# Expert loop of a mixture-of-experts layer: the scaling of the gathered rows moves from VectorE to GpSimd, as a multiplication and an addition

## What is computed

```python
h2 = rms(x, p['g_ffn']) * (1 + sc2) + sh2
aff = softmax(h2 @ w_router)
gate, idx = top_k(swapaxes(aff, 1, 2), cap)        # 64 latent rows, 16 context rows
xg = h2[idx]
a  = xg @ w_e1                                     # 2048 -> 1024
g3 = xg @ w_e3
y  = ((silu(a) * g3) @ w_e2) * gate                # 1024 -> 2048
x  = x + gate2 * zeros.at[idx].add(y)
```

## Time and profile before

| | before |
|---|---|
| median of three runs | 3317.91 us |
| the profiled execution | 3315.78 us |
| its span, first to last instruction | 3313.7 us |
| TensorE busy (share of the span) | 3235.8 us (98%) |
| VectorE busy | 2121.0 us (64%) |
| ScalarE busy | 1391.5 us (42%) |
| GpSimd busy | 358.4 us (11%) |
| granted TensorE clock, mean | 0.991 |

### The profile page before, as it was taken

One profiled execution on the slowest core, in us unless ns is written; L12 is line 12 of the kernel. 1 busy time (PEld: TensorE's weight loads), 2 busy tenths in 40 slices (PEclk: granted clock), 3 DMA queues, 4 the chain that ended last, 5 costly groups with the idle time before them and its releaser, 6 DMA issues. The chain is left out here.

```text
span 3313.7 us, 39738 instructions
## 1 busy us (share of the span) xinstructions
PE 3235.8 (98%) x15947; PEld 2506.7 (76%) x15947; DVE 2121.0 (64%) x1875; ACT 1391.5 (42%) x1271; POOL 358.4 (11%) x445
## 2 busy tenths in 40 slices
PE   7999999999999999999999999969999999999997
PEld 4888888888888999998888888746666666666664
DVE  4355565565552777773233243279999999999997
ACT  3221222221212445452121222247777777777775
POOL 0020010020000000001101112100111111111102
PEclk9999999999999999999999999979999999999999
DMA  9575555485553110125353455379999999999999
GB/s 398 215 230 176 202 178 175 159 271 197 186 187 119 38 48 34 40 101 207 133 172 135 151 172 191 127 256 373 388 398 396 388 384 387 396 393 385 389 391 338
DMA packets 143918, 787.25 MB, mean 238 GB/s; under 512 B 19888, under 2 KB 30672, under 8 KB 63936
## 3 DMA queue, kind: packets, MB, share of 16 engines
q1 hardware_dynamic: 101344, 666.40, 52.2%
q0 software_dynamic: 42448, 119.03, 12.1%
HBM read 718.11 MB, written 67.25 MB: 237 GB/s over the span
## 5 line engine op out<-in xcount | busy, mean ns | idle before, releaser
L102 DVE TENSOR_TENSOR w_lo<-w_stage,w_hi 128x2048 fp32r<-128x2048 f32 x379 | 863.5, 2287 | 95.9 <-ACT w_hi L97 94.7
L97 ACT ACTIVATE w_hi<-w_stage 128x2048 fp32r<-128x2048 f32 x379 | 727.4, 1920 | 299.7 <-PE e_ps L109 299.7
L107 PE MATMUL i_ps<-w_hi,hT_hi 128*128 128x512 f32 (+1 forms) x1440 | 563.0, 391 | 0.1
L109 PE MATMUL i_ps<-w_hi,hT_lo 128*128 128x512 f32 (+1 forms) x1440 | 554.7, 385 | 0.0
L108 PE MATMUL i_ps<-w_lo,hT_hi 128*128 128x512 f32 (+1 forms) x1440 | 554.5, 385 | 0.0
L107 PE MATMUL e_ps<-w_hi,xgT_hi 128*80 128x512 f32 x1024 | 404.3, 395 | 0.0
L108 PE MATMUL e_ps<-w_lo,xgT_hi 128*80 128x512 f32 x1024 | 403.2, 394 | 0.0
L109 PE MATMUL e_ps<-w_hi,xgT_lo 128*80 128x512 f32 x1024 | 400.6, 391 | 0.0
L599 DVE TENSOR_TENSOR w_lo<-w_raw,w_hi 128x2048 fp32r<-128x2048 f32 (+1 forms) x72 | 161.7, 2246 | 345.6 <-ACT w_hi L458 345.6
L107 PE MATMUL p_ps<-w_hi,xT_hi 128*128 128x512 f32 x960 | 377.9, 394 | 1.4 <-DVEq L1841 1.4
L109 PE MATMUL p_ps<-w_hi,xT_lo 128*128 128x512 f32 x960 | 374.1, 390 | 0.0
(11 more groups left out here) (365 smaller groups left out, 4490.9 us busy)
## 6 DMA issues: line engine op xcount, KB each, us to landing
w_stage<-in_w_e SPq DMA_DIRECT2D x384, 1024.0 KB, 7.4
w_stage<-in_w_ada SPq DMA_DIRECT2D x96, 1024.0 KB, 7.1
w_raw<-in_w_in SPq DMA_DIRECT2D x64, 1024.0 KB, 5.0
w_stage<-in_w_o_gm SPq DMA_DIRECT2D x16, 1024.0 KB, 7.4
w_stage<-in_w_o_mla SPq DMA_DIRECT2D x16, 1024.0 KB, 5.1
w_stage<-in_w_out SPq DMA_DIRECT2D x16, 1024.0 KB, 5.0
acts<-evacuated POOLq DMA_DIRECT2D x60, 256.0 KB, 4.4
side<-acts POOLq DMA_DIRECT2D x40, 256.0 KB, 5.5
```

Source lines behind the costliest of these rows:

```text
L97: act.activation(dst, src, ACT.Copy).then_inc(st.hi, 1)
L102: dve.tensor_tensor(dst, src, hi.bitcast(F32), ALU.subtract).then_inc(st.split, 1)
L107: pe.matmul(out, x_hi, w_hi, start=first, stop=False)
L109: return pe.matmul(out, x_lo, w_hi, start=False, stop=last)
```

## The change

VectorE's calls of `rows_scaled` in the loop are removed. GpSimd gets a function of the same name that waits for the gather and then, for each of the three groups of columns, multiplies the rows by their factor (`tensor_scalar`), waits for that, and adds the shift (`tensor_tensor`). It runs after `columns_of(i)` and before `gather(i + 3)`, for experts 2 to 15. TensorE's wait on `x_sc` is as it was. The whole diff:

```diff
--- before.py
+++ after.py
@@ -2063,7 +2063,7 @@
             sem(f"e_{n}") for n in ("x_tr", "x_hi", "x_lo", "sil_ok", "hid_ok", "h_tr", "h_hi", "h_lo", "y_ev"))
         inv, ex, ex_inv, aff_ok, aff_tr, backs, picked, picks, pick_tr, pick_ok = (
             sem(f"r_{n}") for n in ("inv_rows", "ex", "ex_inv", "aff_ok", "aff_tr", "backs", "picked", "picks", "pick_tr", "pick_ok"))
-        shift_in, x_sc, inv_out, issued = sem("r_shift_in"), sem("e_x_scaled"), M.pool_sem("r_inv_out"), sem("r_issued")
+        shift_in, x_sc, x_mul, inv_out, issued = sem("r_shift_in"), sem("e_x_scaled"), sem("e_x_times"), M.pool_sem("r_inv_out"), sem("r_issued")
         f_in, f_out, g_in = [M.pool_sem(f"f_in{b}") for b in range(N_F)], [M.pool_sem(f"f_out{b}") for b in range(N_F)], sem("f_g_in")
         f_sq, f_sum, f_var, f_std, f_inv, f_ok, rows_y_ok, last_out = (
             *(sem(f"f_{n}") for n in ("sq", "sum", "var", "std", "inv", "ok", "rows")), M.pool_sem("last_out"))
@@ -2137,6 +2137,16 @@
                 if e == 0:
                     pool.memset(cur_g[:], 0).then_inc(issued, 1)
 
+            def rows_scaled(e):
+
+                pool_wait(pool, gathered, 16 * e + 16, passed)
+                for g in range(3):
+                    a, b = TXG[g]
+                    c = slice(a * P, b * P)
+                    pool.tensor_scalar(xg[:, c], xg[:, c], xg[:, D:D + 1], None, ALU.mult).then_inc(x_mul, 1)
+                    pool_wait(pool, x_mul, 3 * e + g - 5, passed)
+                    pool.tensor_tensor(xg[:, c], xg[:, c], shift[:, c], ALU.add).then_inc(x_sc, 1)
+
             def columns_of(e):
 
                 pool.tensor_copy(cur_gate[:], gates[:, bass.ds(e, 1)]).then_inc(idx_s, 1)
@@ -2158,10 +2168,13 @@
                 gather_first(e)
             with pool.Fori(0, EXPERTS - 3) as i:
                 columns_of(i)
+                rows_scaled(i + 2)
                 gather(i + 3)
                 scatter(i)
             for e in range(LAST - 2, LAST):
                 columns_of(e)
+                if e + 2 < EXPERTS:
+                    rows_scaled(e + 2)
                 scatter(e)
 
             def load_x(t):
@@ -2368,8 +2381,6 @@
                     lo(n0 + j + LEAD, j + LEAD, i)
                     if j == 8:
                         hidden_lo(i)
-                    if j in (9, 10, 11) and rows:
-                        rows_scaled(i + 2, j - 9)
                     if j == 15:
                         hidden(i + 1)
                     if j == 16 and rows:
```

## The result

The changed kernel takes 3331.15 us (median of five runs, 3330.20 to 3334.54), the kernel before 3317.68 us (five runs, 3317.41 to 3318.12). The ratio is 1.004, 95% interval 1.003 to 1.0051: slower by 13.5 us, 0.4%, a small difference but clear of the noise.

A forecast was written before the change was run, and what follows sets the result against it. TensorE was taken to bound the expert loop. Waits of 1.87 us per expert less 0.56 that disappear gave 1.31, times 14 experts 18.3 us lost: 3336 us as a median, range 3310 to 3360.

The forecast's parts named there:

- All that there is to win: Expert loop: TensorE's 28 waits for VectorE, 7.9 us in all, are the most that the change can gain.
- 0.72 us that are free: Expert loop: a w_lo may be 0.72 us late before TensorE waits, read from two waits of weight loads.
- The price of a pass: GpSimd's new passes: multiplication 0.83 us for 768 columns, 0.61 for 512; addition 1.8 and 1.25.
- What a pass does to w_lo: VectorE's weight subtraction beside GpSimd: a pass that reads SBUF shuts w_lo out for the whole pass.
- The walk: One expert in time order: waits of 0.4, 0.37, 0.8 and 0.3 us, sum 1.87, less 0.56 that disappear.
- The third pair (0.3): Last multiplication and addition of an expert, in the shadow of a later product: 0 to 0.6 us, taken as 0.3.
- GpSimd does not get in between two back-to-back w_lo: VectorE's backlog behind the hidden remainder: GpSimd waits until both w_lo end; the second addition comes in the first gap.
- The rival of the fair turns: Expert loop: GpSimd gets in at every boundary, also in a backlog; 35 us lost, 3353 us; chance 0.13.
- the ring: Three weight-piece slots in the expert loop: ScalarE rounds, VectorE subtracts, TensorE multiplies, then the slot is free again.
- The starved variant: Second addition ends too late, TensorE stands at its transposes some 4 us an expert; 56 us, 3374 us; chance 0.07.
- The sign of being wrong: Next profile: w_lo starting on time during an addition, TensorE's waits below 7.9 us, or the new wait at the transposes.
- the first rival: Expert loop: the passes do not hold up w_lo, so the 7.9 us of waits go; 3310 us; chance 0.15.

The follow-up runs named there:

- none: Kernel before without the scaling of the gathered rows for experts 2 to 15, on either engine: 3316.11 us, ratio 0.9983 to 1.0001.
- spread: Kernel before with VectorE's three passes after steps 2, 4 and 6 instead of 9, 10 and 11, nothing on GpSimd: 3317.90 us.
- the probe: The change plus four multiplications and four additions on otherwise idle GpSimd ahead of the first gather: 3339.72 us in one execution.
- read6: The change with its six GpSimd passes per expert replaced by six copies of 80x2048 from SBUF to an unused tile: 3394.25 us.
- write6: The change with its six GpSimd passes per expert replaced by six fills of 80x2048 that read nothing: 3317.18 us.
- narrow: The change with four groups of 512 columns in place of 768, 768 and 512, same elements, two passes more: 3317.59 us.

## Why the prediction was right, and where its steps were not

The direction, the size (18.3 us forecast, 13.5 measured) and the mechanism held: the additions shut out w_lo for nearly their whole length, and TensorE waits for it. How near the size came is in part luck, as the steps show:

1. **"All that there is to win" is 7.9 us.** Wrong size: 1.8 us (none, spread). The step took the waits of the weight loads as lost time. For the same reason the "0.72 us that are free" are lateness to a waiting load, not to a lost matmul; about 0.23 us more cost no matmul (1.26 us of waiting lost 1.03).
2. **The price of a pass.** The multiplication was put at 0.83 us from the one-input row. It takes 2.21 alone. The sum survived since only its hold counts, 0.62 us. The addition was put at 1.8 and 1.25 us: 1.80 and 1.29 alone, and 1.66 and 1.03 as holds. The estimate of about 1.7 us, scaled from the figure in the Trainium skill (GPSIMD Engine Reference, 3.1), lies within about 0.1 us of both. The Trainium skill (GPSIMD Engine Reference, 4.1) also calls one-input instructions on GpSimd "roughly line-rate"; for a multiplication by a per-partition factor the probe's 2.21 us for 768 columns speak against that, where VectorE did multiplication and addition together in 1.01 us.
3. **What a pass does to w_lo.** "I take the whole pass": right for the additions (holds of 1.57 to 1.66 us of their 1.80), wrong for the multiplications; read6 and write6 show that it is the reading. A copy holds 1.70 us, but what it takes alone was not measured. The one-column copies of the earlier trace rows had shown one half of it.
4. **The walk.** It had four places of waiting worth 1.87 us per expert, which would have raised the waits to about 26 us; there are two, 19.5 us in all, and one of them loses matmul time, 1.03 us. The wait at the first addition (0.4) did not come: w_lo was late by 0.69 only, since the multiplication in front had put it 0.15 late and not 0.4, and the hold was 1.57 and not 1.8. Behind the hidden remainder 0.16 us came instead of 0.37. The second addition was priced at 0.8 and is where the loss is. The third pair (0.3) was absorbed.
5. **"GpSimd does not get in between two back-to-back w_lo"** was wrong for the pass that matters, and it was read from the scatter, which is not a pass. The second addition ran exactly there, ahead of the w_lo of 2493.64. The rival of the fair turns ("GpSimd gets in at every boundary") had the arbitration right for the additions, but not for the multiplications: the third, waiting since 2495.41, did not get in ahead of the w_lo of 2497.50. That rival forecast 35 us because it counted holds of 7.1 us per expert and let the lateness add up, while here the ring had worked off part of each hold before the next. The starved variant had no place: no transpose waited. Why a multiplication waits longer than an addition for its turn stays open.
6. **The sign of being wrong.** "Wrong, if w_lo starts on time while an addition runs": the w_lo of 2487.80 does start on time, inside the addition of 2486.28, and the first rival is wrong all the same. The sign looked at the start of the record, and the hold shows in its length. Neither of the other two signs came: TensorE's waits rose from 7.9 us, and none is at the transposes.

Two errors of size pulled against each other: what the passes cost was forecast as 1.87 us per expert and measured as 1.06 (1.03 of it at the second addition), and what their leaving VectorE gives back was put at 0.56 and measured as 0.13. So 1.87 - 0.56 = 1.31 us were forecast and 1.06 - 0.13 = 0.93 measured; each term was further off than their difference.

## What to carry to other kernels

Before moving work from VectorE to GpSimd, look at what VectorE runs beside it. If that reads two SBUF tensors, expect GpSimd's passes that read SBUF to hold it up, as the additions, multiplications and copies did here; the fills, which only write, did not. What then counts is not the sum of the holds but how late the latest instruction ends (its own hold, plus what earlier ones left) against the slack of the ring behind it, so narrow passes with something between them can be free where wide ones are not. And price a stall by the start-to-start of the matmuls, not by the waits of the weight loads.

## What the runs showed of the hardware that was not expected

- A GpSimd multiplication by a per-partition factor with one tensor input takes longer alone (2.21 us for 80x768, 1.56 for 80x512) than the addition of two tensors (1.80, 1.29), and yet holds up VectorE for 0.62 us only.
- A held VectorE instruction is recorded as longer, not as later: w_lo of 3.94 us instead of 2.28, which starts right behind the one before it. VectorE's busy time rises by what it is held.
- A weight load that waited 0.33 us for its data cost the matmuls under 0.1 us; one that waited 1.26 us cost 1.03.
- Passes differ in when they get their turn between two back-to-back w_lo. Of the passes that began inside a w_lo with the next one close behind it, all 13 additions of the change and 57 of the 58 copies of read6 got in ahead of the next w_lo and stretched it; none of the multiplications did, 15 in the change and 30 in narrow.
